# Rope keys of two cache pages in one tile, and a fourth page slot filled during the prompt attention

## The chip, the cores and the metric

The kernel runs on one core of one Trainium2 chip. Such a core has five engines that work beside each other: TensorE (PE: matmuls, and transposes as matmuls), VectorE (DVE), ScalarE (ACT), GpSimd (POOL) and SyncE (SP), which here issues every DMA. They wait for each other by semaphores. The metric is the device time of one execution in microseconds (us), the median over several runs; lower is better.

## The reference, cut to what matters

Two layers of a hybrid decoder are computed for two groups of requests at once: a prompt of 1024 tokens, and 8 sequences that each add 4 tokens (the "samples") to a past of 1024 tokens. The past lies in a paged cache: rows of 256 latent numbers (used as key and as value) followed by 64 rope numbers (used as key alone), 128 rows to a page, 8 pages to a sequence, which page being given by a table.

```
def mla_attend_sample(qcat, lat, past):
    s_past = jnp.einsum('bqhd,bkd->bhqk', qcat, past) * scale      # 256 latent + 64 rope numbers
    s_new  = jnp.einsum('bqhd,bkd->bhqk', qcat, lat) * scale       # the 4 new tokens, causal
    p = jax.nn.softmax(jnp.concatenate([s_past, s_new], axis=-1), axis=-1)
    o = jnp.einsum('bhqk,bkr->bqhr', p[..., :P], past[..., :KV_RANK])
    return o + jnp.einsum('bhqk,bkr->bqhr', p[..., P:], lat[..., :KV_RANK])

# in layer():
past = cache_mla[l, page_table].reshape(Bs, past_len, LAT_DIM)     # LAT_DIM = 256 + 64
```

Everything is float32. The rest of a layer (input projection, mLSTM, prompt attention, output projection, a convolutional feed-forward part, an embedding gate) is untouched by the change.

## The kernel before, in words

A loop over the two layers runs a fixed row of phases. A phase ends in a barrier of all engines (line 83 and line 91), so what one phase leaves over delays every engine in the next. The phases that matter are `mla_prompt` (attention of the prompt, all PE, ACT and DVE, 32 blocks) and behind it `mla_sample` (attention of the 8 sequences). `out_projection` follows.

The cache stands in DRAM twice over: per page a matrix of 128 partitions by 640 columns. Columns 0 to 383 are the keys with the feature on the partition: latent features 0 to 127, latent features 128 to 255, and a third tile of 128 columns whose upper half holds the 64 rope features and whose lower half is zeros. Columns 384 to 639 are the latents as values, with the row of the page on the partition.

Pages are kept in SBUF in slots, one slot for the 8 pages of one sequence (20 KB per partition). There are five: `pages_0` to `pages_2`, which live through both phases, and `pages_fourth` and `pages_fifth`, which exist in `mla_sample` alone. `load_pages` (line 1117) fills a slot from SP: first 8 page numbers are read from SBUF into registers (line 1119, each one a TENSOR_LOAD, a register operation and a bound check), then one DMA goes out per page (line 1123, each with a register operation for the address before it). SP's program, in its written order, is:

- in `mla_prompt`: slots 0, 1, 2;
- in `mla_sample`: two weights (lines 1346, 1347), slot 3, slot 4; then for sequences 5, 6, 7, each behind a wait on `s_done`, the keys alone into slots 0, 1, 2 (their values are still needed); then for the same three, behind `o_done`, the values alone.

PE works on sequences in two groups of four. Each sequence has 16 query rows (4 tokens by 4 heads) padded to 32, so that four sequences fill the 128 partitions of PSUM, and matmuls of the four quarters run beside each other. For each group: scores (line 1382: two halves c of the row by three key tiles k by four sequences q, 512 columns each, of which the trace records two instructions each), the new tokens' scores (line 1388), a softmax over 1056 columns on DVE and ACT, transposes of the probabilities (line 1398), the product with the values (line 1409), and the way back to heads (lines 1416, 1422). The scores of group 0 wait for slot 3 and for `q_made`, which ACT counts up to 12 while it writes the absorbed queries (`q_absorbed`, lines 1432 and 1436). The scores of group 1 wait for the keys of sequences 4 to 7, and its product with the values for `latents_loaded`, the values of 5 to 7.

Of the kernel before, what the change touches and what calls it, by code (L numbers as in the profile page):

```python
# [45 lines left out]
SCALE = (A_NOPE + A_ROPE) ** -0.5  # L46
NEG = -1.0e30
ROW = N_PAGES * P
TW, VW = 3 * P, KV_RANK
PW = TW + VW  # L50


C_ID, C_PERM, C_ONE, C_ST, C_QK, C_SEL = 0, P, 2 * P, 3 * P, 4 * P, 5 * P
# [98 lines left out]
class Core:  # L152


    def __init__(self, op):
        self.const_in = op["const_in"]
        self.cos_sin = op["cos_sin"]
        self.reset_rows = op["reset_rows"]
        self.x_in = op["x_in"]
        self.p_in = op["p_in"]  # L160
        self.vec_in = op["vec_in"]
        self.final_in = op["final_in"]
        self.w_in = op["w_in"]
        self.w_uq = op["w_uq"]
        self.w_ukv = op["w_ukv"]
        self.w_ukT = op["w_ukT"]
        self.w_out = op["w_out"]
        self.w_up = op["w_up"]
        self.w_down = op["w_down"]
        self.w_gate = op["w_gate"]  # L170
        self.w_proj = op["w_proj"]
        self.cache = op["cache"]
        self.page_table = op["page_table"]
        self.state_in = op["state_in"]
        self.m_in = op["m_in"]
        self.conv_in = op["conv_in"]
        self.y_out = op["y_out"]
        self.lat_out = op["lat_out"]
        self.state_p_out = op["state_p_out"]
        self.state_s_out = op["state_s_out"]  # L180
        self.m_out = op["m_out"]
        self.conv_out = op["conv_out"]


def ds1(i):
    return bass.ds(i, 1)
# [927 lines left out]
                    n += 1  # L1114


def load_pages(sp, core, b, dst, loaded, part=slice(0, PW)):

    ids = [sp.value_load(core.page_ids[0:1, b * N_PAGES + j:b * N_PAGES + j + 1], min_val=0,
                         max_val=core.n_pool - 1) for j in range(N_PAGES)]  # L1120
    for j, page in enumerate(ids):
        src = core.cache[ds1(core.l), ds1(page), :, part].rearrange("l g p n -> (l g p) n")
        sp.dma_start(dst[:, j * PW + part.start:j * PW + part.stop], src).then_inc(loaded, 16)


def mla_expand(nc, core, latp, kn, vt):
# [54 lines left out]
def mla_prompt(nc, core, kr, qn, qr, kn, vt, cat, pages):  # L1181


    with ExitStack() as st:
# [11 lines left out]

        @block.sync
        def _(sp):
            for b in range(3):
                load_pages(sp, core, b, pages[b], ph["pages_loaded"])  # L1200
            sp.wait_ge(ph["pages_loaded"], 3 * N_PAGES * 16)

        @block.tensor
        def _(pe):
# [104 lines left out]
def mla_sample(nc, core, ckv, kr, qn, qr, cat, pages):  # L1309
# [6 lines left out]
    with ExitStack() as st:  # L1316
        def sb(name, shape, dt=F32):
            return st.enter_context(nc.sbuf_tensor(name, shape, dt))
        fourth, fifth = sb("pages_fourth", [P, N_PAGES * PW]), sb("pages_fifth", [P, N_PAGES * PW])
        slots = [pages[0], pages[1], pages[2], fourth, fifth]  # L1320
        SL = len(slots)

        def quarter(q):
            return slice(32 * q, 32 * q + 32)

        def page_slot(b):
            return slots[b % SL][:].rearrange("p (j n) -> p j n", j=N_PAGES)

        ukT = sb("w_uk_T", [P, A_HEADS, KV_RANK])
        uv = sb("w_uv", [P, 2, A_HEADS * A_DV])  # L1330
        qc = sb("q_absorbed", [P, 3, DEC_BATCH, RQ])
        latn = sb("new_latents", [NS, KV_RANK])
        pr = sb("probs_s", [P, ROW + NS])
        pT = sb("probs_s_T", [P, N_PAGES + 1, P])
# [9 lines left out]
        @block.sync  # L1344
        def _(sp):
            sp.dma_start(ukT[:], core.w_ukT[ds1(l)].rearrange("l p h r -> (l p) h r")).then_inc(ph["w_loaded"], 16)
            sp.dma_start(uv[:].rearrange("p k n -> p (k n)"),
                         core.w_ukv[ds1(l), :, 1024:2048].rearrange("l p n -> (l p) n")).then_inc(ph["w_loaded"], 16)
            for b in (3, 4):
                load_pages(sp, core, b, slots[b], ph["pages_loaded"][b])  # L1350
            for b in range(SL, DEC_BATCH):
                sp.wait_ge(ph["s_done"], b - SL + 1)
                load_pages(sp, core, b, slots[b % SL], ph["pages_loaded"][b % SL], slice(0, TW))
            for b in range(SL, DEC_BATCH):
                sp.wait_ge(ph["o_done"], b - SL + 1)
                load_pages(sp, core, b, slots[b % SL], ph["latents_loaded"][b % SL], slice(TW, PW))

        @block.gpsimd
        def _(pool):
# [3 lines left out]
        def _(pe):  # L1363
# [6 lines left out]
            for r in range(2):  # L1370
                tr = pe.transpose(ps[:, 6, r * P:(r + 1) * P], ckv[:, r, NT - P:NT], core.ident)
            tr.then_inc(ph["new_done"], 1)
            pe.wait_ge(ph["q_made"], 12)
            for gr in range(2):
                SB = 3 * gr
                for b in range(max(3, 4 * gr), 4 * gr + 4):
                    pe.wait_ge(ph["pages_loaded"][b % SL], 16 * N_PAGES)
                for c in range(2):
                    for k in range(3):
                        for q in range(4):  # L1380
                            b = 4 * gr + q
                            pe.matmul(ps[quarter(q), SB + c, :].rearrange("p (j n) -> p j n", j=4),
                                      qc[:, k, b, :], page_slot(b)[:, 4 * c:4 * c + 4, k * P:(k + 1) * P],
                                      start=(k == 0), stop=(k == 2))
                for k in range(3):
                    for q in range(4):
                        src = ckv[:, k, SEQ:NT] if k < 2 else kr[:, SEQ:NT]
                        mm = pe.matmul(ps[quarter(q), SB + 2, 0:NS], qc[:, k, 4 * gr + q, :], src,
                                       start=(k == 0), stop=(k == 2))
                        if k == 2:  # L1390
                            mm.then_inc(ph["s_done"], 1)
                pe.wait_ge(ph["stepd"], 5 * gr + 5)
                if gr:
                    pe.wait_ge(ph["pt_made"], 3)
                else:
                    pe.wait_ge(ph["new_made"], 1)
                for j in range(N_PAGES):
                    tr = pe.transpose(ps[:, 6 + j // 4, (j % 4) * P:(j % 4 + 1) * P],
                                      pr[:, j * P:(j + 1) * P], core.ident)
                    if j % 4 == 3:  # L1400
                        tr.then_inc(ph["tr_done"], 1)
                pe.matmul(ps[0:NS, SB + 1, 0:P], pr[:, ROW:ROW + NS], core.ident, start=True, stop=True)\
                  .then_inc(ph["tr_done"], 1)
                pe.wait_ge(ph["pt_made"], 3 * gr + 3)
                for b in range(max(SL, 4 * gr), 4 * gr + 4):
                    pe.wait_ge(ph["latents_loaded"][b % SL], 16 * N_PAGES)
                for j in range(N_PAGES):
                    for q in range(4):
                        pe.matmul(ps[quarter(q), SB, 0:VW], pT[:, j, quarter(q)],
                                  page_slot(4 * gr + q)[:, j, TW:PW], start=(j == 0), stop=False)  # L1410
                for q in range(4):
                    pe.matmul(ps[quarter(q), SB, 0:VW], pT[0:NS, N_PAGES, quarter(q)], latn[:],
                              start=False, stop=True).then_inc(ph["o_done"], 1)
                pe.wait_ge(ph["o_made"], gr + 1)
                for r in range(2):
                    tr = pe.transpose(ps[:, SB + 2, r * P:(r + 1) * P], o[:, r * P:(r + 1) * P], core.ident)
                tr.then_inc(ph["oT_done"], 1)
                pe.wait_ge(ph["oT_made"], gr + 1)
                for h in range(A_HEADS):
                    for r in range(2):  # L1420
                        src = oT[:, r, :].rearrange("p (b n) -> p b n", b=4)[:, :, 4 * h:4 * h + 4]
                        mm = pe.matmul(ps[:, SB, h * 16:(h + 1) * 16].rearrange("p (b n) -> p b n", b=4),
                                       uv[:, r, h * A_DV:(h + 1) * A_DV], src, start=(r == 0), stop=(r == 1))
                mm.then_inc(ph["ha_done"], 1)

        @block.scalar
        def _(act):
            act.wait_ge(ph["ql_done"], 1)
            act.wait_ge(ph["zeroed"], 1)
            for h in range(A_HEADS):  # L1430
                for r in range(2):
# [1 line left out]
                                   ps[:, 7, (2 * h + r) * NS:(2 * h + r + 1) * NS]  # L1433
                                   .rearrange("p (b t) -> p b t", b=DEC_BATCH), ACT.Copy)\
                       .then_inc(ph["q_made"], 1)
                act.activation(qc[0:A_ROPE, 2, :, 4 * h:4 * h + 4],
                               qr[part(h), h // 2, SEQ:NT].rearrange("p (b t) -> p b t", b=DEC_BATCH),
                               ACT.Copy).then_inc(ph["q_made"], 1)
            act.wait_ge(ph["new_done"], 1)
            act.activation(latn[:], ps[P - NS:P, 6, 0:2 * P], ACT.Copy).then_inc(ph["new_made"], 1)  # L1440
            for gr in range(2):
# [523 lines left out]
def build_program(nc, operands, n_pool):  # L1965
# [4 lines left out]
    with ExitStack() as whole:  # L1970
# [16 lines left out]
        with nc.Fori(0, DEPTH) as l:  # L1987
# [3 lines left out]
            with ExitStack() as mix:  # L1991
# [28 lines left out]
                with queries:  # L2020
                    prompt = ExitStack()
                    with ExitStack() as s1:
                        latp = keep(s1, "lat_parts", [P, 2, 2, NT], F32R, side="right")
                        with latent, ExitStack() as s2:
                            cqp = keep(s2, "cq_parts", [P, 2, 3, NT], F32R)
                            mla_queries(nc, core, cq, ckv, kr, cqp, latp, qn, qr)
                        pages = [keep(mix, f"pages_{i}", [P, N_PAGES * PW]) for i in range(2)]
                        kn = keep(prompt, "a_k", [P, A_HEADS, SEQ])
                        vt = keep(prompt, "a_v", [P, SEQ // P, A_HEADS * A_DV])
                        mla_expand(nc, core, latp, kn, vt)  # L2030
                    pages.append(keep(queries, "pages_2", [P, N_PAGES * PW], side="right"))
                    with prompt:
                        mla_prompt(nc, core, kr, qn, qr, kn, vt, cat, pages)
                    mla_sample(nc, core, ckv, kr, qn, qr, cat, pages)
# [170 lines left out]
```

## Time and profile before

| | us |
|---|---|
| median of 3 runs | 3756.83 |
| lowest, highest | 3756.39, 3762.57 |
| the profiled execution, whole | 3760.17 |
| its span, first to last instruction | 3757.8 |
| PE busy (matmuls) | 3207.4 (85%) |
| DVE, ACT, POOL busy | 1587.5, 1056.6, 86.2 |

The whole time of the profiled execution is 2.4 us above its span. Its mean granted TensorE clock is 0.887 of full speed. The profile shows PE and its weight loads (PEld), the compute engines, and SPq, the issue of DMAs by SP; register instructions and page number loads of SP are not counted as busy, so that SP has to be read from the places where its DMAs start. A row's idle time is that of the engine just before the instruction, with what released it. Wherever a share of busy time is quoted, it is a mean over stages with different limits.

### The profile page before, as it was taken

What the parts mean: (1) busy time and instruction counts of PE and PEld (TensorE: products, weight loads), DVE (VectorE), ACT (ScalarE), POOL (GpSimd) and SP (SyncE); (2) the same over time, 40 slices, a digit from 0 to 9 for tenths busy, and PEclk for the clock granted to TensorE, in tenths of its full rate; (3) what the DMA queues carried; (4) which work ended last, traced back from release to release, by engine and by line L of the source; (5) the groups of instructions that cost most, each with busy time, mean ns of one, the idle gap of its engine ahead of it and who ended that gap; (6) DMA issues with size and microseconds to landing.
All of it is one profiled execution on the core that took longest, in us unless ns stands there. A gap on an engine that the chain in (4) does not pass through costs nothing. (4 is left out here: it accounts for less than half of the span.)

```text
span 3757.8 us, 49080 instructions
## 1 busy us (share of the span) xinstructions
PE 3207.4 (85%) x19116; PEld 2937.1 (78%) x19116; DVE 1587.5 (42%) x2506; ACT 1056.6 (28%) x1957; POOL 86.2 (2%) x216
## 2 busy tenths in 40 slices
PE   4987669848999999997979686796689999999987
PEld 4985465438999999996979665554579999999976
DVE  4004434323644544547330243342255454454474
ACT  3222123212433233234222221232223323323341
POOL 0000000000000000000000000000000000000000
PEclk9995569969999999998989855898789999999998
DMA  5200112150111111102131001023311111111023
GB/s 199 74 1 1 47 50 85 63 180 27 57 46 46 46 45 46 46 23 78 41 124 49 1 1 67 30 85 103 140 39 56 46 45 46 46 45 46 16 85 122
DMA packets 58324, 224.72 MB, mean 60 GB/s; under 512 B 6634, under 2 KB 22506, under 8 KB 42994
## 3 DMA queue, kind: packets, MB, share of 16 engines
q1 hardware_dynamic: 58098, 221.46, 16.3%
q8 instruction: 171, 2.80, 0.3%
q14 instruction: 55, 0.45, 0.0%
HBM read 193.92 MB, written 27.52 MB: 59 GB/s over the span
## 5 line engine op out<-in xcount | busy, mean ns | idle before, releaser
L147 PE MATMUL psum<-h_parts_ffn,conv_ffn_weight_parts 128*128 128x352 f32 x2112 | 683.9, 324 | 38.2 <-DVE h_parts_ffn L231 30.8
L148 PE MATMUL psum<-h_parts_ffn,conv_ffn_weight_parts 128*128 128x352 f32 x2112 | 679.3, 322 | 0.0
L149 PE MATMUL psum<-h_parts_ffn,conv_ffn_weight_parts 128*128 128x352 f32 x2112 | 679.2, 322 | 0.0
L1724 DVE SCALAR_TENSOR_TENSOR conv_sum<-u_padded,vectors,conv_sum 128x1024 f32<-128x1024 f32 x176 | 226.1, 1285 | 577.2 <-ACT conv_sum L1674 564.7
L147 PEld LDWEIGHTS psum<-h_parts_ffn,conv_ffn_weight_parts 128*128 128x128 f32 x2112 | 397.9, 188 | 41.8 <-issue 38.9
L148 PEld LDWEIGHTS psum<-h_parts_ffn,conv_ffn_weight_parts 128*128 128x128 f32 x2112 | 398.3, 189 | 0.0
L149 PEld LDWEIGHTS psum<-h_parts_ffn,conv_ffn_weight_parts 128*128 128x128 f32 x2112 | 398.0, 188 | 0.0
L147 PE MATMUL psum<-g_parts,conv_ffn_weight_parts 128*128 128x352 f32 x1056 | 346.0, 328 | 27.3 <-DVE g_parts L1735 16.3
L149 PE MATMUL psum<-g_parts,conv_ffn_weight_parts 128*128 128x352 f32 x1056 | 343.8, 326 | 0.0
L148 PE MATMUL psum<-g_parts,conv_ffn_weight_parts 128*128 128x352 f32 x1056 | 343.6, 325 | 0.0
L1743 DVE TENSOR_TENSOR x<-x,psum 128x352 f32<-128x352 f32 x528 | 255.6, 517 | 120.0 <-PE psum L149 119.6
L1670 ACT ACTIVATE u_padded<-psum 128x352 f32<-128x352 f32 (+1 forms) x264 | 120.6, 457 | 523.0 <-PE psum L149 523.0
L147 PEld LDWEIGHTS psum<-g_parts,conv_ffn_weight_parts 128*128 128x128 f32 x1056 | 200.4, 190 | 33.7 <-DVE x L1743 16.8
L147 PE MATMUL psum<-h_parts,_projection_weight_parts 128*128 128x352 f32 x576 | 187.8, 326 | 28.4 <-DVE h_parts L231 28.3
L148 PEld LDWEIGHTS psum<-g_parts,conv_ffn_weight_parts 128*128 128x128 f32 x1056 | 200.4, 190 | 0.0
L149 PEld LDWEIGHTS psum<-g_parts,conv_ffn_weight_parts 128*128 128x128 f32 x1056 | 199.6, 189 | 0.0
L148 PE MATMUL psum<-h_parts,_projection_weight_parts 128*128 128x352 f32 x576 | 186.1, 323 | 0.0
L149 PE MATMUL psum<-h_parts,_projection_weight_parts 128*128 128x352 f32 x576 | 185.8, 323 | 0.0
L1683 ACT ACTIVATE g_parts<-conv_sum 128x1056 fp32r<-128x1056 f32 x44 | 47.8, 1087 | 487.0 <-PE psum L149 404.6
L141 DVE TENSOR_TENSOR _projection_weight_parts<-_projection_weight_stage,_projection_weight_parts 128x2048 fp32r<-128x2048 f32 x26 | 59.5, 2290 | 285.7 <-ACT _projection_weight_parts L135 285.7
L1674 ACT ACTIVATE conv_sum<-psum,vectors 128x352 f32<-128x352 f32 x264 | 170.8, 647 | 0.0
L141 DVE TENSOR_TENSOR conv_ffn_weight_parts<-conv_ffn_weight_stage,conv_ffn_weight_parts 128x2048 fp32r<-128x2048 f32 x66 | 151.1, 2289 | 23.0 <-ACT conv_ffn_weight_parts L135 23.0
(303 smaller groups left out, 5709.0 us busy)
## 6 DMA issues: line engine op xcount, KB each, us to landing
conv_ffn_weight_stage<-w_up_dram SPq DMA_DIRECT2D x44, 1024.0 KB, 4.8
conv_ffn_weight_stage<-w_down_dram SPq DMA_DIRECT2D x22, 1024.0 KB, 4.9
_projection_weight_stage<-w_in_dram SPq DMA_DIRECT2D x18, 1024.0 KB, 5.0
pages<-cache_dram SPq DMA_DIRECT2D x48, 320.0 KB, 4.8
pages<-cache_dram SPq DMA_DIRECT2D x48, 192.0 KB, 3.0
x_tiles<-x_residual SPq DMA_DIRECT2D x16, 528.0 KB, 3.6
x<-x_residual SPq DMA_DIRECT2D x2, 4224.0 KB, 16.3
x_residual<-x SPq DMA_DIRECT2D x16, 528.0 KB, 2.7
```

Of the source, the lines that this page charges most:

```text
L141: dve.tensor_tensor(dst[:, 1, 0:width], self.stage[:, slot, 0:width], dst[:, 0, 0:width].bitcast(F32), ALU.subtract).then_inc(self.ph["lo_ ...
L147: pe.matmul(out, lhs[0], rhs[0], start=first, stop=False)
L148: pe.matmul(out, lhs[0], rhs[1], start=False, stop=False)
L149: return pe.matmul(out, lhs[1], rhs[0], start=False, stop=last)
L1670: act.activation(u[:, q, 2 + c * CH:2 + c * CH + n], src[:, 0:n], ACT.Copy)
L1674: op = act.activation(t[:, q, chunk(c)], src, ACT.Identity, bias=bias, scale=w2)
L1683: act.activation(gp[:, 0, slot, :], t[:, 1, :], ACT.Copy).then_inc(ph["ghi_made"], 1)
L1724: dve.scalar_tensor_tensor(t[:, q, 0:SEQ], row[:, tap:tap + SEQ], w, t[:, q, 0:SEQ], ALU.mult, ALU.add).then_inc(ph["conv_step"], 1)
L1743: dve.tensor_tensor(X[:, k, chunk(c)], X[:, k, chunk(c)], ps[:, (6 + n) % 8, 0:CH], ALU.add).then_inc(ph["x_made"], 1)
```

## The change

The third key tile is no longer padded with zeros. The cache is given in two tensors: `cache` with 512 columns per page (two key tiles of 128 and the 256 value columns), and `cache_rope` with 64 partitions by 128 columns per page. In SBUF the rope keys of an even page go to partitions 0 to 63 and those of the next odd page to partitions 64 to 127 of one tile behind the pages, four such tiles to a slot, so that a slot takes 18 KB per partition. Each page whose keys are loaded now has two DMAs.

In the scores, k runs to 4. Steps 0 and 1 are as before; steps 2 and 3 multiply the shared rope tile with a query tile that holds the rope query in partitions 0 to 63 and zeros below (step 2, even pages), or zeros above and the rope query in 64 to 127 (step 3, odd pages). They write every second block of 128 columns, so 256 columns each. ACT writes four more small tiles (`q_made` goes to 16), and `q_absorbed` is cleared at 1024 columns per partition in place of 768.

There are still five slots, but four of them (`pages_0` to `pages_3`) exist already in `mla_prompt` and are filled there. In `mla_sample` SP fills only the fifth before the waits.

```
-TW, VW = 3 * P, KV_RANK
-PW = TW + VW
+KW, VW = KV_RANK, KV_RANK
+MW = KW + VW
+PW = N_PAGES * MW + N_PAGES // 2 * P
...
-def load_pages(sp, core, b, dst, loaded, part=slice(0, PW)):
+def load_pages(sp, core, b, dst, loaded, keys=True, values=True):
...
     ids = [sp.value_load(core.page_ids[0:1, b * N_PAGES + j:b * N_PAGES + j + 1], min_val=0,
                          max_val=core.n_pool - 1) for j in range(N_PAGES)]
+    lo, hi = 0 if keys else KW, MW if values else KW
     for j, page in enumerate(ids):
-        src = core.cache[ds1(core.l), ds1(page), :, part].rearrange("l g p n -> (l g p) n")
-        sp.dma_start(dst[:, j * PW + part.start:j * PW + part.stop], src).then_inc(loaded, 16)
+        src = core.cache[ds1(core.l), ds1(page), :, lo:hi].rearrange("l g p n -> (l g p) n")
+        sp.dma_start(dst[:, j * MW + lo:j * MW + hi], src).then_inc(loaded, 16)
+        if keys:
+            at = N_PAGES * MW + j // 2 * P
+            src = core.cache_rope[ds1(core.l), ds1(page)].rearrange("l g p n -> (l g p) n")
+            sp.dma_start(dst[part(j), at:at + P], src).then_inc(loaded, 16)
...
-            for b in range(3):
+            for b in range(len(pages)):
                 load_pages(sp, core, b, pages[b], ph["pages_loaded"])
-            sp.wait_ge(ph["pages_loaded"], 3 * N_PAGES * 16)
+            sp.wait_ge(ph["pages_loaded"], len(pages) * 2 * N_PAGES * 16)
...
-            for b in (3, 4):
+            for b in range(len(pages), SL):
                 load_pages(sp, core, b, slots[b], ph["pages_loaded"][b])
             for b in range(SL, DEC_BATCH):
                 sp.wait_ge(ph["s_done"], b - SL + 1)
-                load_pages(sp, core, b, slots[b % SL], ph["pages_loaded"][b % SL], slice(0, TW))
+                load_pages(sp, core, b, slots[b % SL], ph["pages_loaded"][b % SL], values=False)
             for b in range(SL, DEC_BATCH):
                 sp.wait_ge(ph["o_done"], b - SL + 1)
-                load_pages(sp, core, b, slots[b % SL], ph["latents_loaded"][b % SL], slice(TW, PW))
+                load_pages(sp, core, b, slots[b % SL], ph["latents_loaded"][b % SL], keys=False)
...
-            pe.wait_ge(ph["q_made"], 12)
+            pe.wait_ge(ph["q_made"], 16)
             for gr in range(2):
                 SB = 3 * gr
-                for b in range(max(3, 4 * gr), 4 * gr + 4):
-                    pe.wait_ge(ph["pages_loaded"][b % SL], 16 * N_PAGES)
+                for b in range(max(len(pages), 4 * gr), 4 * gr + 4):
+                    pe.wait_ge(ph["pages_loaded"][b % SL], 2 * 16 * N_PAGES)
                 for c in range(2):
-                    for k in range(3):
+                    for k in range(4):
                         for q in range(4):
                             b = 4 * gr + q
-                            pe.matmul(ps[quarter(q), SB + c, :].rearrange("p (j n) -> p j n", j=4),
-                                      qc[:, k, b, :], page_slot(b)[:, 4 * c:4 * c + 4, k * P:(k + 1) * P],
-                                      start=(k == 0), stop=(k == 2))
+                            s = ps[quarter(q), SB + c, :].rearrange("p (j n) -> p j n", j=4)
+                            if k < 2:
+                                pe.matmul(s, qc[:, k, b, :], page_slot(b)[:, 4 * c:4 * c + 4, k * P:(k + 1) * P],
+                                          start=(k == 0), stop=False)
+                            else:
+                                pe.matmul(s[:, k - 2::2, :], qc[:, k, b, :], rope_slot(b)[:, 2 * c:2 * c + 2, :],
+                                          start=False, stop=(k == 3))
...
-                act.activation(qc[0:A_ROPE, 2, :, 4 * h:4 * h + 4],
-                               qr[part(h), h // 2, SEQ:NT].rearrange("p (b t) -> p b t", b=DEC_BATCH),
-                               ACT.Copy).then_inc(ph["q_made"], 1)
+                for i in range(2):
+                    act.activation(qc[part(i), 2 + i, :, 4 * h:4 * h + 4],
+                                   qr[part(h), h // 2, SEQ:NT].rearrange("p (b t) -> p b t", b=DEC_BATCH),
+                                   ACT.Copy).then_inc(ph["q_made"], 1)
...
-                    pages.append(keep(queries, "pages_2", [P, N_PAGES * PW], side="right"))
+                    pages += [keep(queries, f"pages_{i}", [P, PW], side="right") for i in (2, 3)]
```

How the instructions stand is shown at two places. The first is SP in `mla_sample` where the keys of sequence 5 are loaded again into slot 0: before, the last of the eight page numbers and the first two pages (ISA rows are register operations and the bound check; `pages_0` is the slot).

```order
L1119 TENSOR_LOAD page_ids
L1119 ISA x2
L1123 ISA
L1123 DMA pages_0<-cache_dram 128x384
L1123 ISA
L1123 DMA pages_0<-cache_dram 128x384
```

The same place of SP after the change:

```order
L1122 TENSOR_LOAD page_ids
L1122 ISA x2
L1127 ISA
L1127 DMA pages_0<-cache_dram 128x256
L1131 ISA
L1131 DMA pages_0<-cache_rope_dram 64x128
L1127 ISA
L1127 DMA pages_0<-cache_dram 128x256
L1131 ISA
L1131 DMA pages_0<-cache_rope_dram 64x128
```

The page number loads are as many as before; behind each page's DMA stands a second pair of a register operation and a DMA, 8 pairs to a slot, in all slots and in the three key reloads, and none in the three value reloads.

The second place is PE at the start of the scores of group 0 (the transposes of new latents, then the first score steps; each row is a matmul of the program). Before:

```order
L1371 MATMUL psum<-constants,ckv 128x128 x2
L1382 MATMUL psum<-pages_0,q_absorbed 32x512 [waits pages_loaded_3,q_made_0]
L1382 MATMUL psum<-pages_1,q_absorbed 32x512
L1382 MATMUL psum<-pages_2,q_absorbed 32x512
L1382 MATMUL psum<-pages_fourth,q_absorbed 32x512
```

After the change, there and on to the first shared rope tile:

```order
L1381 MATMUL psum<-constants,ckv 128x128 x2
L1394 MATMUL psum<-pages_0,q_absorbed 32x512 [waits q_made_0]
L1394 MATMUL psum<-pages_1,q_absorbed 32x512
L1394 MATMUL psum<-pages_2,q_absorbed 32x512
L1394 MATMUL psum<-pages_3,q_absorbed 32x512
L1394 MATMUL psum<-pages_0,q_absorbed 32x512
L1394 MATMUL psum<-pages_1,q_absorbed 32x512
L1394 MATMUL psum<-pages_2,q_absorbed 32x512
L1394 MATMUL psum<-pages_3,q_absorbed 32x512
L1397 MATMUL psum<-pages_0,q_absorbed 32x2x128
```

The wait for a page load is gone from the first score matmul; it waits for the absorbed queries alone. The third step of each half has become two steps of half the columns.

## Rows read from the trace of the kernel before

**Rows 1.** The page, its head: busy time of each engine over the span.
```profile
span 3757.8 us, 49080 instructions
PE 3207.4 (85%) x19116; PEld 2937.1 (78%) x19116; DVE 1587.5 (42%) x2506; ACT 1056.6 (28%) x1957; POOL 86.2 (2%) x216
```

**Rows 2.** Stretches: length, PE, PEld, DVE, ACT, POOL busy, PEclk, DMA share, GB/s.
```profile
744.90:752.30 7.40, 7.21 (x72) 2.25 (x72) 0.00 (x0) 0.00 (x0) 0.00 (x0) 0.77 0.98 336
752.30:782.50 30.20, 10.47 (x100) 6.31 (x100) 3.19 (x7) 3.04 (x6) 0.00 (x0) 0.66 0.51 161
797.00:809.50 12.50, 0.44 (x7) 0.27 (x11) 0.00 (x0) 0.00 (x0) 0.00 (x0) 0.50 0.43 127
```

**Rows 3.** What SP waited for, 728 to 820 us: total, times, longest.
```profile
SPq L91 <- PEq L91: 117.3, 2, 105.3
SPq L1119 <- PE psum L1388: 4.1, 1, 4.1
```

**Rows 4.** Timeline, SP, `mla_sample`, layer 1: start, us over all xcount issues.
```profile
734.87 4.30 SPq L1123 DMA_DIRECT2D pages_fourth<-cache_dram  x8
766.16 4.29 SPq L1123 DMA_DIRECT2D pages<-cache_dram  x8
775.13 4.28 SPq L1123 DMA_DIRECT2D pages<-cache_dram  x8
802.74 4.41 SPq L1123 DMA_DIRECT2D pages<-cache_dram  x8
```

**Rows 5.** Timeline, PE, where it takes up work again in layer 1.
```profile
744.96 1.07 PE L1382 MATMUL psum<-pages,q_absorbed 128*32 128x512 f32 x3 [7.03 <-DMA pages_fourth<-cache_dram]
782.54 1.03 PE L1382 MATMUL psum<-pages_fifth,q_absorbed 128*32 128x512 f32 x1 [14.14 <-DMA pages<-cache_dram]
809.06 0.61 PE L1409 MATMUL psum<-pages_fifth,probs_s_T 128*32 128x256 f32 x1 [12.57 <-DMA pages<-cache_dram]
```

**Rows 6.** Instructions of two SP lines: ns min/median/max, first and last start.
```profile
L1119 SPq TENSOR_LOAD <-page_ids x176: 261/267/473, 589.0 to 2655.6; - x176
L1123 SPq FUSED_REGOPS  x176: 86/86/122, 593.6 to 2660.2; - x176
L1123 SPq DMA_DIRECT2D pages<-cache_dram x144: 332/333/542, 593.9 to 2660.4; - x144
```

**Rows 7.** Tiles `m_first` (4 partitions) and `k_rope` (64), SP: ns min/median/max.
```profile
L513 SPq DMA_DIRECT2D m_first<-m_in_dram x2: 258/264/269, 270.4 to 2123.5; - x2
L990 SPq DMA_DIRECT2D lat_out_dram<-k_rope x2: 579/580/582, 517.5 to 2370.6; - x2
```

**Rows 8.** Timeline, POOL and ACT, the absorbed queries, layer 1.
```profile
728.82 0.74 POOL L1360 MEMSET q_absorbed<- 128x768 f32 x1 [253.46 <-POOLq L83]
738.48 0.23 ACT L1436 ACTIVATE q_absorbed<-a_q_rope 64x32 f32<-64x32 f32 x1
738.89 0.23 ACT L1436 ACTIVATE q_absorbed<-a_q_rope 64x32 f32<-64x32 f32 x1
```

**Rows 9.** Timeline, PE, score and value steps, the first three about a clock change.
```profile
747.49 1.05 PE L1382 MATMUL psum<-pages,q_absorbed 128*32 128x512 f32 x3
748.34 0.62 PE L1382 MATMUL psum<-pages,q_absorbed 128*32 128x512 f32 x3
748.78 0.61 PE L1382 MATMUL psum<-pages,q_absorbed 128*32 128x512 f32 x3
762.58 0.39 PE L1409 MATMUL psum<-pages,probs_s_T 128*32 128x256 f32 x3
762.79 0.39 PE L1409 MATMUL psum<-pages,probs_s_T 128*32 128x256 f32 x3
```

**Rows 10.** Timeline: SP in `mla_prompt`, and ACT and PE in layer 2.
```profile
593.85 23.15 SPq L1123 DMA_DIRECT2D pages<-cache_dram  x24
2592.42 0.23 ACT L1436 ACTIVATE q_absorbed<-a_q_rope 64x32 f32<-64x32 f32 x1
2598.85 1.07 PE L1382 MATMUL psum<-pages,q_absorbed 128*32 128x512 f32 x3 [7.39 <-DMA pages_fourth<-cache_dram]
```

More of the change, by code:

```diff
@@ L172, in __init__ @@
         self.cache = op["cache"]
+        self.cache_rope = op["cache_rope"]
         self.page_table = op["page_table"]
@@ L1318, in sb @@
             return st.enter_context(nc.sbuf_tensor(name, shape, dt))
-        fourth, fifth = sb("pages_fourth", [P, N_PAGES * PW]), sb("pages_fifth", [P, N_PAGES * PW])
-        slots = [pages[0], pages[1], pages[2], fourth, fifth]
+        slots = pages + [sb("pages_last", [P, PW])]
         SL = len(slots)
@@ L1326, in page_slot, with rope_slot @@
         def page_slot(b):
-            return slots[b % SL][:].rearrange("p (j n) -> p j n", j=N_PAGES)
+            return slots[b % SL][:, 0:N_PAGES * MW].rearrange("p (j n) -> p j n", j=N_PAGES)
+        def rope_slot(b):
+            return slots[b % SL][:, N_PAGES * MW:PW].rearrange("p (j n) -> p j n", j=N_PAGES // 2)
         ukT = sb("w_uk_T", [P, A_HEADS, KV_RANK])
         uv = sb("w_uv", [P, 2, A_HEADS * A_DV])
-        qc = sb("q_absorbed", [P, 3, DEC_BATCH, RQ])
+        qc = sb("q_absorbed", [P, 4, DEC_BATCH, RQ])
         latn = sb("new_latents", [NS, KV_RANK])
@@ L1409, in _ @@
                         pe.matmul(ps[quarter(q), SB, 0:VW], pT[:, j, quarter(q)],
-                                  page_slot(4 * gr + q)[:, j, TW:PW], start=(j == 0), stop=False)
+                                  page_slot(4 * gr + q)[:, j, KW:MW], start=(j == 0), stop=False)
                 for q in range(4):
@@ L2026, in build_program @@
                             mla_queries(nc, core, cq, ckv, kr, cqp, latp, qn, qr)
-                        pages = [keep(mix, f"pages_{i}", [P, N_PAGES * PW]) for i in range(2)]
+                        pages = [keep(mix, f"pages_{i}", [P, PW]) for i in range(2)]
                         kn = keep(prompt, "a_k", [P, A_HEADS, SEQ])
@@ L2140 @@
     n_pool = cache.shape[1]
-    cache_T = np.zeros((L, n_pool, P, 3, PAGE), np.float32)
     cT = cache.transpose(0, 1, 3, 2)
-    cache_T[:, :, :, 0] = cT[:, :, 0:P]
-    cache_T[:, :, :, 1] = cT[:, :, P:2 * P]
-    cache_T[:, :, 0:A_ROPE, 2] = cT[:, :, 2 * P:]
     state = np.zeros((L, P, DEC_BATCH, 2, DV1), np.float32)
@@ L2160 @@
         "w_gate": tiles(w["ple_w_gate"], 256), "w_proj": tiles(w["ple_w_proj"], D_MODEL)[:, 0],
-        "cache": np.concatenate([cache_T.reshape(L, n_pool, P, TW), cache[..., 0:VW]], 3),
+        "cache": np.concatenate([cT[:, :, 0:P], cT[:, :, P:2 * P], cache[..., 0:VW]], 3),
+        "cache_rope": cT[:, :, 2 * P:],
         "page_table": w["page_table"].reshape(1, -1).astype(np.int32),
```

## The prediction

> **What bounds the kernel now.** I read five views, in this order. The page's head [rows 1] says that PE is busy 85% of the span. That is a mean over all stages and says nothing of `mla_sample`, so I went to the stretches of that phase. There PE is nearly idle twice: in 752.3 to 782.5 it is busy 10.5 of 30.2 us, in 797.0 to 809.5 it is busy 0.4 of 12.5 us [rows 2]. PE's own rows name what it waited for: a page DMA each time, 7.0 us ahead of the scores of group 0 (slot 3), 14.1 us ahead of the scores of group 1 (the reloaded keys), 12.6 us ahead of the product of group 1 with its values [rows 5].
>
> A DMA can be late because the data moves slowly or because it was issued late. SP's rows answer that. From 728 to 820 us SP waited once inside the phase, 4.1 us for the scores of group 0 (`s_done`) [rows 3]; after that it never waits. A key reload of one slot repeats every 775.13 - 766.16 = 8.97 us: 4.3 us in which 8 DMAs go out, and 4.7 us in which 8 page numbers are read [rows 4]. A step of DMA issue is (4.29 - 0.33)/7 = 0.566 us, made of the DMA instruction of 0.333, the address operation of 0.086 [rows 6] and the gaps about them. The last key DMA is issued by 775.13 + 4.28 = 779.4, PE starts at 782.5; the last value DMA by 802.74 + 4.41 = 807.15, PE starts at 809.06 [rows 4, 5]. So from `s_done` at about 752.2, where the stretch of the scores ends [rows 2], to 807.2, the end of this phase hangs on SP's instruction stream: three key reloads and three value reloads, one behind the other. That is the chain to cost. What PE, DVE and ACT do for group 1 lies inside it: they are through at 797, and wait.
>
> **A gain: the fourth slot is there already.** Scores of group 0 no longer wait for slot 3, but for the absorbed queries. The last of them starts at 738.89 and takes 0.23, so 739.12 [rows 8]. The change puts four more such copies on ACT. Three copies of a head take 738.89 - 738.48 = 0.41 us [rows 8], so a fourth costs between 0.14 and its full 0.23, over four heads 0.55 to 0.9; I take 0.65 and a start at 739.8. Against 744.96 [rows 5] that is 5.2 us earlier. In layer 2 the last copy ends at 2592.65 and scores begin at 2598.85 [rows 10]: 5.5 us by the same working. The larger clearing of `q_absorbed` (0.74 us from 728.8, by columns 1.0) ends long before ACT writes there [rows 8]; it costs nothing.
>
> The scores then run a stretch of changing clock. PE stood idle for 7.0 us before them; the first four steps of 512 columns come 0.85 us apart (half clock, 1.2 GHz), from 748.34 on they come 0.43 apart (2.4 GHz) [rows 9]. When the clock rises after an earlier start, no row tells. With all twelve steps at the high level the scores take 4 x 0.42 = 1.7 us less than now, with all at the low level 8 x 0.42 = 3.4 us more. The ends are far apart and nothing lies nearer to either, so I take their middle, +0.85 us per layer.
>
> The rope steps themselves change nothing in this sum: two steps of 256 columns stand for one of 512, and steps of 256 columns come 0.21 us apart at the high clock where those of 512 come 0.43 apart [rows 9]. That the output is written in every second block of 128 columns has no row; bounds are nothing, and one more step of 0.43 for each of the two halves, 0.9 us. I take nothing, since columns, not blocks, set the row that is there.
>
> **A loss: twice the DMAs in the key reloads.** Each of the three key reloads has 8 more pairs of address operation and DMA, and the same 8 page numbers. SP is free of the fifth slot in time: it issues its first slot from 734.87 on [rows 4], now with 16 DMAs of 0.566, so until 743.9, before `s_done` comes at about 752.2 - 5.2 + 0.85 = 747.9. Then 24 x 0.566 = 13.6 us are added on the chain. No row shows a DMA into 64 partitions from a register address. The nearest are the page DMAs themselves, which take 0.33 whether they move 320, 192 or 128 KB [rows 4, 6]; below lies a DMA into 4 partitions, 0.26; above one from 64 partitions, 0.58, which stands right behind a large one [rows 7]. With the 0.23 of address work and gaps that makes 0.49 to 0.81 for each, 11.8 to 19.4 us per layer. I take 0.566, the price of its neighbours in the same loop.
>
> Here the Trainium skill (DMA: Bandwidth & Descriptors, Rules for kernel authors) speaks against the edit: it advises to coalesce many small transfers, calls those under 64 KB mostly overhead, and says that two transfers to disjoint partition halves gain nothing over one transfer. The rope tiles are 32 KB each, to alternating halves. The trace agrees on the main point: 192 KB and 128 KB cost SP the same. By bytes alone the sum would be a gain (the first rival), by count it is the loss above.
>
> The value reloads keep 8 DMAs each (256 columns as before). They begin when SP is through with the keys and do not wait for `o_done` now or then; their landing, 1.9 us behind the last issue, is unchanged. So the shift of SP at the end of the keys is the shift of the phase. The smaller key DMAs may land sooner (3.1 us between last issue and PE now, 1.9 for values of 128 KB), but that only gives PE an earlier start of group 1, whose cover is large: 797 - 782.5 = 14.5 us of work against the 9.1 x 3 of the value reloads.
>
> **Nothing in the prompt attention.** SP's loads there begin at 589.0 [rows 6]; 24 DMAs spread over 23.15 us [rows 10], and then SP waits 105.3 us for PE [rows 3]. Added are one slot (4.7 + 4.3) and 32 rope DMAs at 0.566 (18.1), 27 us in 105. If that cover were gone the phase would be longer by what sticks out; it is far from it. The bytes fall from 320 to 288 KB per page, on engines that are no bound there.
>
> **The sum.** Layer 1: 13.6 - 5.2 + 0.85 = +9.25 us. Layer 2: 13.6 - 5.5 + 0.85 = +8.95. Together +18.2 us, on 3760.17 of the profiled execution: 3778.4. The median of the runs stands 3.3 us below that execution, so the forecast is 3756.83 + 18.2 = 3775.0.
>
> **Rivals.** *Bytes, not issues, bind (ends faster).* While slot 4 is loaded the DMA engines are busy 0.98 of the time at 336 GB/s [rows 2], and key DMAs of 192 KB at 0.566 us would be 347 GB/s, the same rate. If the pitch is the engines' and not SP's, a page of 160 KB takes 160/192 of 0.566, and three reloads save 3 x 8 x 0.094 = 2.3 us, beside the earlier start: 2 x (-2.3 - 5.35 + 0.85) = -13.6 us, 3743. Against it: values of 128 KB come at (4.41 - 0.33)/7 = 0.58 us, no faster, at 127 GB/s and a DMA share of 0.43 over their stretch. It decides only if a rope DMA costs SP less than (5.35 - 0.85)/24 = 0.19 us, below the 0.26 of the smallest DMA seen. 4%.
>
> *Rope DMAs are cheap to issue.* If the second address operation and the shorter list run at 0.35 us in all, the loss is 8.4 per layer, and the sum 2 x (8.4 - 4.5) = +8, 3764.6. For it: the 0.26 of rows 7. Against: then the gaps, which stand at every DMA, would have to shrink too. 8%, half of it within 0.2%.
>
> *Rope DMAs are dear.* At 0.81 each, by the 64-partition row of 0.58: 2 x (19.4 - 4.5) = +29.8, 3786.6. Against it: that row moves 64 rows of 1056 columns right behind a larger DMA, and these move 128 columns each. 13%.
>
> *The early slot brings nothing.* If something else holds the scores of group 0 (the absorbed queries late, SP still busy with the fifth slot when `s_done` comes), the loss stands alone: 2 x 13.6 = +27, 3784. Against it: SP's 4 us of slack worked out above, and queries at 739.1. 7%.
>
> **How the numbers follow.** Forecast (issue price within 0.5 to 0.7, the gain as worked out): 68%, from 3767 to 3782. Range: its low end is 11.8 - 5.35 - 1.7 = 4.75 per layer, +9.5, 3766; its high end holds the two dear cases in most of their width, 3790. A change under 0.2% (7.5 us) is about what a measurement of this kernel can't tell from none. Faster by more than that: the first rival, 3%. Within it: the rest of that rival, half of the cheap case and some of the forecast's low edge, 7%. Slower: 90%.
>
> **What would show it.** In the profile after: scores of group 0 start about 739.8 in layer 1, released by ACT and not by a DMA (if not, the gain is wrong). SP's key reloads repeat every 8.97 + 8 x 0.566 = 13.5 us (if 9, the loss is). PE's wait ahead of the scores of group 1 grows from 14.1 to 26 or 27 us, and that ahead of the values stays near 13. `mla_sample` ends about 9 us later after its start, in both layers, and SP still waits over 70 us at the end of `mla_prompt`. The forecast is wrong if SP, after `s_done`, is found waiting, or if stages outside this phase change by more than a few us.

## The result, and the profile after

| us | before | after |
|---|---|---|
| median | 3758.6 (4 runs) | 3792.8 (4 runs) |
| lowest, highest | 3756.4, 3762.6 | 3788.5, 3796.7 |
| the profiled execution, whole | 3760.2 | 3796.7 |
| its span | 3757.8 | 3794.8 |

The ratio is 1.009, with a 95% interval of 1.0072 to 1.0107: slower by 34.2 us, where 18.2 was forecast and 3790 was the top of the range. The direction was right, the size was not.

The head of the page after, against [rows 1]: the busy time of every engine has hardly moved.

```profile
span 3794.8 us, 49598 instructions
PE 3211.9 (85%) x19180; PEld 2942.0 (78%) x19180; DVE 1587.4 (42%) x2506; ACT 1058.8 (28%) x1965; POOL 86.6 (2%) x216
```

So 37 us were added in which engines stand idle. The starts of the phases, set beside those of before, say where: `mla_sample` is 17.3 us longer in layer 1 and 17.8 in layer 2; all other phases together make 2 us, a few up and a few down by 1 to 3 us each.

What PE waited for in `mla_sample` of layer 1, from the view of waits (total, times, longest):

```profile
PE psum L1394 <- DMA pages<-cache_rope_dram: 31.5, 1, 31.5
PE psum L1423 <- DMA pages<-cache_dram: 14.4, 1, 14.4
```

The wait for slot 3 is gone, that for the reloaded keys has grown from 14.1 to 31.5 us [rows 5] (26 or 27 were forecast), that for the values from 12.6 to 14.4. SP waited as before, in the same view of SP:

```profile
SPq L92 <- PEq L92: 90.6, 2, 76.4
SPq L1122 <- PE psum L1402: 3.4, 1, 3.4
```

It waited once inside the phase, 3.4 us for `s_done` (4.1 in [rows 3]), and 76.4 us for PE at the end of the prompt attention in place of 105.3. The prompt's loads took 29 us more and stay hidden. Both are as forecast. The timeline of SP, first DMA of the first and of the second key reload, and two pages from the middle of the second:

```profile
755.04 0.34 SPq L1127 DMA_DIRECT2D pages<-cache_dram  x1
...
770.50 0.34 SPq L1127 DMA_DIRECT2D pages<-cache_dram  x1
771.08 0.47 SPq L1131 DMA_DIRECT2D pages<-cache_rope_dram  x1
771.78 0.40 SPq L1127 DMA_DIRECT2D pages<-cache_dram  x1
772.41 0.47 SPq L1131 DMA_DIRECT2D pages<-cache_rope_dram  x1
773.12 0.40 SPq L1127 DMA_DIRECT2D pages<-cache_dram  x1
```

A reload repeats after 770.50 - 755.04 = 15.46 us, not 13.5 as forecast and 8.97 in [rows 4]. A page takes 773.12 - 771.78 = 1.34 us, where twice the old step would be 1.13. The rope DMA holds SP for 0.47 us, and the key DMA, which took 0.33 in [rows 6], now takes 0.40; the first key DMA of a reload, which has page number loads ahead of it and no rope DMA, takes 0.34. The group view of all such DMAs gives the same:

```profile
L1127 SPq DMA_DIRECT2D pages<-cache_dram x160: 332/393/1129, 592.9 to 2694.2; - x160
L1131 SPq DMA_DIRECT2D pages<-cache_rope_dram x112: 474/475/1537, 593.5 to 2666.0; - x112
```

PE's return to work, and the stretch from the first value product to the end of the phase (PEclk is the third number from the end):

```profile
743.29 1.08 PE L1394 MATMUL psum<-pages,q_absorbed 128*32 128x512 f32 x4 [2.69 <-ACT q_absorbed L1451]
```

```profile
826.20:838.50 12.30, 10.61 (x90) 6.64 (x90) 0.65 (x2) 0.38 (x1) 0.00 (x0) 0.64 0.01 1
```

Counted from the clearing of `q_absorbed` (728.82 before [rows 8], 730.65 after), which opens the phase, the chain reads as follows in layer 1, with layer 2 in brackets where it differs by more than 0.2:

| us from the phase's start | before | after | one DMA per page (e1) | both full width (e4) |
|---|---|---|---|---|
| scores of group 0 start | 16.1 | 12.6 (12.1) | 12.2 (11.4) | 12.8 |
| SP: first key DMA | 28.0 | 24.4 | 24.3 (23.8) | 24.6 |
| SP: last key DMA out | 50.6 | 65.7 | 46.9 (46.4) | 61.1 |
| SP: last value DMA out | 78.3 | 93.5 | 74.6 (74.1) | 88.8 |
| values on PE start | 80.2 | 95.6 (95.8) | 76.6 (76.2) | 90.8 |
| last copy of the phase | 90.1 (89.8) | 107.4 (107.6) | 86.5 (86.2) | 100.4 |

### The profile page after: what moved, and what is told of

The parts are those of the page before. It is cut to its first block and busy times, and to the rows that moved or that the text cites. A ratio compares the mean times of both kernels' runs of the same rounds, so it can differ in the third digit from the quotient of the medians.

```text
span 3794.8 us, 49598 instructions
## 1 busy us (share of the span) xinstructions
PE 3211.9 (85%) x19180; PEld 2942.0 (78%) x19180; DVE 1587.4 (42%) x2506; ACT 1058.8 (28%) x1965; POOL 86.6 (2%) x216
```

## The experiments

**e1: one DMA per page, early fourth slot kept.** The rope keys of a page need 64 partitions by 128 columns. Laid out as 128 partitions by 64 columns, they sit beside the two key tiles and come with the page's one DMA. The two rope steps then take the first and the second 64 keys of every page, 256 columns each as in the changed kernel.

```
+KW, VW = KV_RANK + A_ROPE, KV_RANK         # key columns: 128, 128, 64
...
-            src = core.cache_rope[...]; sp.dma_start(dst[part(j), at:at + P], src)
...
-    pe.matmul(s[:, k - 2::2, :], qc[:, k, b, :], rope_slot(b)[:, 2 * c:2 * c + 2, :], ...)
+    pe.matmul(s[:, :, (k - 2) * A_ROPE:(k - 1) * A_ROPE], qc[:, k, b, :],
+              page_slot(b)[:, 4 * c:4 * c + 4, 2 * P:KW], ...)
```

> The rope keys of a page are laid out as 128 partitions by 64 columns (features of keys 0 to 63 above, of keys 64 to 127 below) beside the two key tiles, so that a page's keys come with one DMA; rope steps, slot size and the early fourth slot stay as in the changed kernel. Theory (the loss is the count of DMAs that SP issues in the key reloads): the reload of a slot takes 9 us again, not 15.1, and only the gain of the early slot is left, 3.6 us per layer as the profile of the changed kernel shows it: 3758.6 - 7 = 3751. Rival (the rope steps on PE, or their strided output, cost): the loss stays in part, the kernel is slower than before, 3765 or more.

Measured: 3748.6 us (7 runs) against 3757.8 of before on the same chip, ratio 0.9973 (0.9962 to 0.9984). This is faster than before by 9.2 us and than the changed kernel by 44. SP's reloads are back at 8.96 us:

```profile
763.59 4.28 SPq L1126 DMA_DIRECT2D pages<-cache_dram  x8
...
772.55 4.28 SPq L1126 DMA_DIRECT2D pages<-cache_dram  x8
```

The rival falls: the two rope steps cost nothing that shows. The steps of e1 write blocks of 64 columns and those of the changed kernel every second block of 128; for the latter the changed kernel's own trace speaks, where the score steps of group 0 in layer 1 took 6.9 us against 7.0 before. The loss is the second DMA.

**e2: one DMA per page, fourth slot late.** As e1, with

```
-        slots = pages + [sb("pages_last", [P, PW])]
+        slots = pages + [sb("pages_fourth", [P, PW]), sb("pages_last", [P, PW])]
...
-                    pages += [... for i in (2, 3)]
+                    pages += [... for i in (2,)]
```

> As the kernel with one DMA per page, but the fourth slot is loaded in the sample phase as before the change. Theory: with neither the second DMA nor the early slot nothing is left of the change but four ACT copies that are hidden behind the load of slot 4: 3758, same as before within 3 us, and 7 us above the kernel with one DMA and the early slot. Rival (early slot brings nothing): no difference between the two.

Measured: 3756.7 us (11 runs), ratio 0.9998 (0.9989 to 1.0007). Same as before, and 8.1 us above e1. So the early slot is worth 8 us over two layers, and a tenth fewer bytes per page (288 KB in place of 320) is worth nothing that shows.

**e3: shared rope tiles with two DMAs per page, fourth slot late.** The changed kernel with the two edits of e2.

> The changed kernel with its fourth slot loaded in the sample phase: the shared rope tiles with two DMAs per page alone. Theory (SP's instruction stream): scores of group 0 wait for 16 DMAs of slot 3, 6 us later than in the changed kernel, and SP is busy with slot 4 until 32 us into the phase while the scores are done at 26, so the reloads begin 12 us later than in the changed kernel: 3793 + 25 = 3818. Rival (the DMA engines' bandwidth is what counts): the two slots have fewer bytes than before the change, and the kernel is within 8 us of the changed one.

Measured: 3811.0 us (4 runs), ratio 1.014 (1.0125 to 1.0156), 18 us above the changed kernel, where the rival allowed 8. The rival is out: bytes are fewer than before the change, and the time is 53 us longer. The 25 of the expectation were too many by 7. In the trace scores of group 0 start 6.1 us later than in the changed kernel and are done at 26, the next reload's DMAs begin at 36.8 behind slot 4, 12.4 later, as expected. The whole phase is but 10.1 us longer, because the end of it is 2.3 us shorter than in the changed kernel (9.5 us from the first value product to the last copy, against 11.8). That difference is taken up below.

**e4: two DMAs per page, both 128 partitions wide.** The changed kernel, still with `cache_rope` as a tensor of its own, but in the 128 by 64 layout of e1:

```
-            sp.dma_start(dst[part(j), at:at + P], src).then_inc(loaded, 16)          # 64 x 128
+            sp.dma_start(dst[:, at:at + A_ROPE], src).then_inc(loaded, 16)           # 128 x 64
```

> Two DMAs per page as in the changed kernel, from the same two DRAM tensors in turn, but the rope DMA moves 128 partitions by 64 columns in place of 64 partitions by 128. The changed kernel's rope DMA holds SP for 0.474 us and the key DMA beside it for 0.394, where every page DMA before took 0.333. Theory A (the shape of 64 partitions is dear): both fall to 0.333, the pair from 1.335 to 1.13 us, 24 pairs 4.9 us per layer: 3783. Theory B (taking turns between two DRAM tensors is dear): durations and time as in the changed kernel, 3793.

Measured: 3776.7 us (4 runs), ratio 1.0044 (1.0029 to 1.006). Bytes, tensors, their order and the number of DMAs are those of the changed kernel; the price of an issue is the old one:

```profile
770.23 0.33 SPq L1127 DMA_DIRECT2D pages<-cache_dram  x1
770.79 0.33 SPq L1131 DMA_DIRECT2D pages<-cache_rope_dram  x1
771.36 0.33 SPq L1127 DMA_DIRECT2D pages<-cache_dram  x1
```

771.36 - 770.23 = 1.13 us for a pair. Theory A holds, theory B falls. This kernel, in which the second DMA has the price that I gave it, is 18.9 us above before, and I had forecast 18.2 for the change. That the totals agree so well is in part luck. The DMAs added 13.9 us per layer from the first key DMA to the last (13.6 forecast), but `mla_sample` became 10.4 and 10.7 us longer, not 9.25 and 8.95, since the gain was smaller than forecast; the other phases of the profiled execution made up for it with 3 us less.

**e5: what a shape costs the issuing engine.** In e1's prompt attention SP has spare time, so groups of four DMAs were put there:

```
+            for rows, width in ((128, 128), (96, 128), (64, 128), (64, 64), (64, 256), (32, 128), (16, 128), (4, 128)):
+                for i in range(4):
+                    sp.dma_start(scratch[0:rows, i * 256:i * 256 + width], w[0:rows, i * 256:i * 256 + width])
+                (wait for the four)
```

> The kernel with one DMA per page, and in the prompt attention, where SP waits some 90 us for PE, groups of four DMAs each from a weight's rows (never contiguous) into a scratch tile nobody reads: 128, 96, 64, 64, 64, 32, 16 and 4 partitions by 128, 128, 128, 64, 256, 128, 128 and 128 columns, each group behind the landing of the one before, then four that take turns between 128 and 64 partitions, then four of 128 partitions that take turns between two DRAM tensors. Theory (64 partitions are a dear shape for the issuing engine, whatever the source): the 64-partition groups take about 0.47 us an issue at any width, 128 partitions 0.33, turns between tensors 0.33. Rival (the contiguous source or the turns between tensors made the rope DMA dear): 64 partitions 0.33 like 128, and the last group above it.

Measured: 3752.3 us (one run); what counts are the rows of SP. The timeline, one row per group, in the order of the list, then the turns between 128 and 64 partitions (L1217) and between two tensors (L1222, first two of four):

```profile
630.64 1.88 SPq L1211 DMA_DIRECT2D scratch<-w_up_dram  x4
634.17 1.74 SPq L1211 DMA_DIRECT2D scratch<-w_up_dram  x4
637.80 2.50 SPq L1211 DMA_DIRECT2D scratch<-w_up_dram  x4
641.90 3.11 SPq L1211 DMA_DIRECT2D scratch<-w_up_dram  x4
646.43 2.39 SPq L1211 DMA_DIRECT2D scratch<-w_up_dram  x4
650.83 1.72 SPq L1211 DMA_DIRECT2D scratch<-w_up_dram  x4
653.90 1.94 SPq L1211 DMA_DIRECT2D scratch<-w_up_dram  x4
657.00 1.34 SPq L1211 DMA_DIRECT2D scratch<-w_up_dram  x4
659.39 2.13 SPq L1217 DMA_DIRECT2D scratch<-w_up_dram  x4
663.18 0.33 SPq L1222 DMA_DIRECT2D scratch<-w_up_dram  x1
663.71 0.33 SPq L1222 DMA_DIRECT2D scratch<-w_down_dram  x1
```

Four issues take 1.88 us at 128 partitions, 1.74 at 96, and 2.4 to 3.1 at 64, whether 64, 128 or 256 columns wide (the 3.11 holds one stray issue of 1.27). At 32, 16 and 4 partitions they take 1.72, 1.94 and 1.34 (the 1.94 holds a stray issue of 0.61). The single issues behind the first of a group are 0.33, 0.37, 0.55, 0.37, 0.37 and 0.25 us for 128, 96, 64, 32, 16 and 4 partitions. So 64 is the dear case among these, not one on a line from small to large. The width doesn't make it so, nor does a source without gaps, since these sources have gaps. Of the four issues that take turns between two tensors the third took 0.38, in both layers, and the others in layer 1 0.33; e4, where 24 pairs take turns at 0.33, shows that such a turn is not what cost 0.47. My expectation had 0.47 for each at 64 partitions; back to back it is 0.47 for the first of a group in two of the three groups (0.59 in the other) and 0.55 for the next. Where shapes take turns, the one issue of 128 partitions behind one of 64 took 0.54. Why 64 is dear no run here tells.

**e6: keys first, rope DMAs behind them.** The changed kernel with the two DMAs of a page in two loops:

```
     for j, page in enumerate(ids):  sp.dma_start(dst[:, j * MW + lo:j * MW + hi], src) ...
+    for j, page in enumerate(ids if keys else []):
+        sp.dma_start(dst[part(j), at:at + P], src).then_inc(loaded, 16)
```

> The changed kernel, with the eight key DMAs of a slot issued first and its eight rope DMAs behind them. Theory (the key DMA pays 0.06 because a 64-partition DMA stands ahead of it): the key DMAs fall to 0.333, the rope DMAs stay at 0.47, a reload gets 0.5 us shorter. Rival (a page's key DMA of 1 KB rows pays for something else): it stays at 0.39.

Measured: 3785.0 us (one run). Timeline of SP, second key reload:

```profile
770.01 4.30 SPq L1127 DMA_DIRECT2D pages<-cache_dram  x8
774.54 5.38 SPq L1131 DMA_DIRECT2D pages<-cache_rope_dram  x8
```

The key DMAs are back at (4.30 - 0.33)/7 = 0.57 us a step, the rope DMAs stand at (5.38 - 0.47)/7 = 0.70. A reload repeats after 15.0 us, 0.4 less than in the changed kernel. Key DMAs were dearer there because of the DMA that stood ahead of them. The single time, 8 us below the changed kernel's median, fits a phase that is 3.4 us shorter; 1.1 of that is SP's, and 2.2 are again at the end of the phase.

**e7: SP relieved.** In e1, the value reloads of two sequences are issued by ACT, which is idle between the groups:

```
                 act.activation(oT[:], ...).then_inc(ph["oT_made"], 1)
+                if gr == 0:
+                    for b in range(SL, DEC_BATCH - 1):
+                        act.wait_ge(ph["o_done"], b - SL + 1)
+                        load_pages(act, core, b, slots[b % SL], ph["latents_loaded"][b % SL], keys=False)
```

SP keeps the values of sequence 7.

> The kernel with one DMA per page, and the value reloads of sequences 5 and 6 issued by ACT between its work for group 0 and group 1, sequence 7 by SP behind the keys. Theory (the issue on SP is what the values of group 1 wait for, not the transfers): ACT issues from 38 to 56 us of the phase, SP has the last values out by 58, and PE goes from scores over softmax to the values without a stall at about 65 in place of 76.6: 12 us less per layer, 3748 - 24 = 3724. Rival (transfers or DRAM are the limit): loads of both engines take turns, the values land no earlier, 3745 or more.

Measured: 3726.0 us (5 runs) against 3758.6, ratio 0.9912 (0.9898 to 0.9926), the fastest kernel of this study, 32.6 us below before. PE now goes to the values without a DMA in the way:

```profile
795.07 0.64 PE L1416 MATMUL psum<-pages_last,probs_s_T 128*32 128x256 f32 x1 [0.36 <-ACT probs_s_T L1465]
```

It waited 12.6 us there before [rows 5]. The same bytes move; what has changed is who issues them, and that 16 of the 24 value DMAs go out on ACT from 38.6 us of the phase on, beside SP's last key reload. The rival is out.

## Why the prediction was right and wrong

**The bound was read rightly.** "The end of this phase hangs on SP's instruction stream": SP did not wait after `s_done`, PE's waits follow it, halving the DMAs (e1) takes the loss away, and giving some to ACT (e7) takes away a wait that was there before. The rival by which bytes bind is refuted by e3 and e4.

**The step that failed: the price of a rope DMA.** I took 0.566 us each, "the price of its neighbours in the same loop", and put the dear case at 13%. From the first key DMA to the last, before took 50.59 - 27.99 = 22.6 us and after 65.75 - 24.39 = 41.4, so 24 rope DMAs added 18.8 us, 0.78 each, where I had 13.6. Of the 0.22 that I missed, 0.14 is the rope DMA itself (0.474 against 0.333) and 0.06 is the key DMA behind it (0.394). The row for 64 partitions stood in [rows 7] with 0.58, and I explained it away: it "stands right behind a large one". That was misread, and the trace of before could have settled it. The timeline of SP has the two 6.7 us apart:

```profile
510.81 0.36 SPq L987 DMA_DIRECT2D lat_out_dram<-ckv  x1
517.49 0.58 SPq L990 DMA_DIRECT2D lat_out_dram<-k_rope  x1
```

The large one held SP for 0.36 us and had landed after 4.0, before the other was issued. e4 and e5 show for loads that 64 partitions are the dear case; no run varies this store. The second half, that a dear DMA makes the next one dearer, was in no row of before. Over two layers the price is 2 x 5.2 = 10.4 us of what is missing.

What came is the rival "rope DMAs are dear", which had 13% and 0.81 for each. Even its sum, 3786.6, falls 6 us short of the median, for the most part by the next two terms. The edges were loosely worked out, too. The top of the range, 3790, is no sum of its bounds: the dear price with the scores at the low level gives 2 x (19.4 - 5.35 + 3.4) = 34.9, 3791.7. And 3767, the low edge of the forecast, needs the price of 0.5 with the scores at the high level, 2 x (12.0 - 5.35 - 1.7) = 9.9, while 3782 has the middle of that term.

**The gain was mis-sized.** Scores of group 0 started 3.5 us earlier in layer 1 and 4.2 in layer 2, not 5.2 and 5.5. About half of the miss in layer 1 is ACT. The timeline of ACT, two heads of four:

```profile
740.33 0.47 ACT L1451 ACTIVATE q_absorbed<-a_q_rope 64x32 f32<-64x32 f32 x2
740.83 0.28 ACT L1446 ACTIVATE q_absorbed<-psum 128x32 f32<-128x32 f32 x2
741.13 0.48 ACT L1451 ACTIVATE q_absorbed<-a_q_rope 64x32 f32<-64x32 f32 x2
741.63 0.29 ACT L1446 ACTIVATE q_absorbed<-psum 128x32 f32<-128x32 f32 x2
```

A head takes 0.80 us where it took 0.41 [rows 8]. I had bounded the added copy by its full 0.23. But the copy behind such a pair starts only when the pair is over (741.13 + 0.48, and 741.63), where before the copy behind a single one from `a_q_rope` (738.48 [rows 8]) started 0.14 us after it:

```profile
738.62 0.26 ACT L1432 ACTIVATE q_absorbed<-psum 128x32 f32<-128x32 f32 x2
```

That makes some 0.8 us of the miss, over four heads. The rest is that PE's first product started 0.8 us later in the phase (0.5 in layer 2); in layer 1 the weight `w_uv` was also issued 0.35 us later. Why, I did not find out. Of my clock term, +0.85, nothing came in layer 1, where the score steps took 6.9 us against 7.0, and 0.55 in layer 2, 7.34 against 6.79. `s_done` came 3.6 us earlier in both layers, where 4.35 and 4.65 were forecast. That is a miss of 1.8 us in all.

**A term I did not have: the clock at the phase's end.** From the first value product to the last copy the changed kernel takes 11.8 us, before 9.8, e1 9.9, e3 9.5, e4 9.7, e6 9.6. Its granted clock over that stretch is 0.64, where 0.79 stood before. Both times PE came from a wait of over 12 us for a DMA. In the changed kernel it then worked for 5.5 us at 1.2 GHz, was granted 2.4 GHz for 3.4 us, and finished at 1.2 GHz; before, it worked for 4.1 us at 1.2 GHz and had 2.4 GHz up to the end of the phase. The stretches (PEclk is the third number from the end), after and before:

```profile
826.20:831.74 5.54, 5.54 (x53) 2.90 (x57) 0.00 (x0) 0.00 (x0) 0.00 (x0) 0.50 0.01 3
831.74:835.15 3.41, 2.26 (x30) 1.04 (x22) 0.42 (x1) 0.38 (x1) 0.00 (x0) 1.00 0.00 0
835.15:838.22 3.07, 2.81 (x14) 2.70 (x13) 0.22 (x1) 0.00 (x0) 0.00 (x0) 0.50 0.00 0
```

```profile
809.06:813.20 4.14, 4.14 (x40) 2.21 (x44) 0.00 (x0) 0.00 (x0) 0.00 (x0) 0.50 0.02 4
813.20:819.11 5.91, 4.50 (x54) 2.88 (x46) 0.64 (x2) 0.38 (x1) 0.00 (x0) 1.00 0.00 0
```

So there are two parts, a later rise and an early fall. The last product with `w_uv` shows the level at the very end, after and before:

```profile
834.73 3.23 PE L1436 MATMUL psum<-o_latent_T,w_uv 128*128 128x16 f32 x16 [0.47 <-ACT o_latent_T L1475]
```

```profile
816.89 1.96 PE L1422 MATMUL psum<-o_latent_T,w_uv 128*128 128x16 f32 x16 [0.47 <-ACT o_latent_T L1460]
```

It costs 2.0 us per layer, 4 us in all, in the one execution of this kernel that was profiled. The waits ahead of the values are nearly equal in e3, e4 and e6 (13.5 to 13.8 us, here 14.4), and these kernels don't pay it: there the clock rose after 3.4 to 3.8 us and stayed up to the end of the phase. What sets the moments of the rise and of the fall stays open. Together, 10.4 of the price, 1.8 of the gain, 4 of the clock, 0.4 of the values' landing and 2 us from other phases make 18.6. The spans of the two profiled executions differ by 37.0, so 37.0 - 18.2 = 18.8 are to be explained. Between the medians it is 34.2 - 18.2 = 16; the profiled execution was the slowest of the four.

**What was hidden stayed hidden.** The prompt attention's loads ended 76 us before PE. The values landed 2 us behind their last issue, as before. Two rope steps of 256 columns cost PE what one of 512 had cost, as e2 shows in the time.

## What to carry to other kernels

Where a queue of small DMAs sets the end, count its instructions and time one from start to start; here the bytes that they moved did not decide. Before splitting a transfer to save zeros, look for a layout that keeps one full-width transfer: with the fourth slot early in both, the same 288 KB per page gave 9 us of gain in one DMA and 34 us of loss in two. And take a row of the same shape at its word, rather than the rows of the same loop. If something seems to explain it away, such as a large DMA ahead of it, look up in the timeline how far ahead that stood.

## What the runs showed of the hardware

- The time that a load holds SP is not monotone in its partitions: back to back 0.33 us for 128, 0.37 for 96, 0.55 for 64, 0.37 for 32 and 16, 0.25 for 4, and independent of the row width from 256 bytes to 1 KB at 64 partitions (e5). With an address operation between them, loads of 64 partitions took 0.47 each (e6).
- Part of that price falls on the next DMA: one of 128 partitions took 0.39 to 0.40 in place of 0.33 us behind one of 64 when an address operation stood between them (the changed kernel), 0.54 with nothing between (e5), and the old 0.33 once the two kinds were grouped (e6).
- Taking turns between two DRAM tensors cost nothing over 24 pairs per layer (e4: 0.33 for each).
- Behind waits of 12.6 to 14.4 us for a DMA, matmuls of PE ran at 1.2 GHz for 3.4 to 5.5 us before 2.4 GHz was granted, by kernel (layer 1 of e3 3.4, e6 3.7, e4 3.8, before 4.1, e1 4.4, the changed kernel 5.5).
- ACT issues such DMAs at about SP's rate, 16 in 13.3 us with the page numbers between, and both queues ran beside each other: PE did not wait for the values, and the scores of group 1 started some 0.5 us later than in e1 (e7).
